# Sixteen more weight panels in block two by seven half-size products, weight sums made by adding transfers in DRAM

## The reference

```python
h = rms_norm_2(x, norm_g)
proj = h @ w_in                      # 1024 -> 4 branches and 4 x 1024 gates
y_a = chunked_spatial_gating(a_u, a_v, ...) * jax.nn.silu(a_z)
y_b = dsa_attention(b_q, b_c, b_qi, b_ki, b_wi, ...) * jax.nn.silu(b_z)
y_c = short_gated_conv(c_b, c_c, c_x, conv_w) * jax.nn.silu(c_z)
y_d = forgetting_attention(d_q, d_k, d_v, d_f, fox_b_f) * jax.nn.silu(d_z)
branch_d = jnp.einsum('nbsw,nwd->bsnd', jnp.stack([y_a, y_b, y_c, y_d]), w_branch)
g = jax.nn.sigmoid(gates.reshape(bsz, s, 4, d))
x + jnp.sum(g * branch_d, axis=2) @ w_out      # then a last rms norm
```

## Time and profile before

| | |
|---|---|
| median of 3 runs | 1111.67 us (1111.41 to 1111.82) |
| span of the profiled execution | 1109.4 us, 18066 instructions (its own time beyond the span is not on the page) |
| PE | 7344 matmuls, 1100.7 us busy |
| PEld | 931.1 us |
| DVE | 1195 instructions, 744.2 us busy |
| ACT | 851 instructions, 506.9 us busy |
| POOL | 40 instructions, 19.8 us busy |
| TensorE clock granted | 0.999 of full speed over the span |
| DMA | 121.09 MB, 109 GB/s as a mean |
| queue of SP (q1) | 109.88 MB, its packets took 29.7% of 16 engines' span |
| queue of POOL (q0) | 10.03 MB, 2.7% |

### The profile page before, as it was taken

The page is one execution under the profiler, slowest core; times in us unless marked ns, Lnnn a source line. Parts: engine busy times, 40 slices in busy tenths (PEclk is TensorE's granted clock), DMA queues, the critical chain, the costliest instruction groups (busy, mean ns, idle before and its releaser), DMA issues.

```text
span 1109.4 us, 18066 instructions
## 1 busy us (share of the span) xinstructions
PE 1100.7 (99%) x7344; PEld 931.1 (84%) x7344; DVE 744.2 (67%) x1195; ACT 506.9 (46%) x851; POOL 19.8 (2%) x40
## 2 busy tenths in 40 slices
PE   9999999999999999999999999999999999999997
PEld 8888888888888888878888887887789999999986
DVE  6875876864686247448789896447568677667853
ACT  7562354324675225533342434336544444444543
POOL 1000000000001001000000000000000000000000
PEclk9999999999999999999999999999999999999999
DMA  9543324432215433522223232231121322333241
GB/s 372 220 149 125 125 68 133 127 102 73 74 58 167 139 95 111 185 74 79 77 76 95 77 95 68 66 114 58 58 73 61 114 93 80 115 115 114 81 186 76
DMA packets 33618, 121.09 MB, mean 109 GB/s; under 512 B 3824, under 2 KB 3824, under 8 KB 33536
## 3 DMA queue, kind: packets, MB, share of 16 engines
q1 hardware_dynamic: 30672, 109.88, 29.7%
q0 software_dynamic: 2720, 10.03, 2.7%
q10 hardware_dynamic: 144, 0.03, 0.0%
HBM read 115.74 MB, written 4.19 MB: 108 GB/s over the span
## 4 chain that ended last, share of the span: by engine, by line
PE 98%; DMA 1%; DVE 1%; ACT 0%; SPq 0%; issue 0%; ACTq 0%
PE acc L1829 22%; PE acc L1831 21%; PE acc L1830 21%; PE acc L1841 2%; PE side L1841 2%; PE acc L1839 2%; PE side L1839 2%; PE acc L1837 2%; PE side L1837 2%; PE acc L2189 2%; PE side L1829 2%; PE side L1830 2%; PE side L1831 2%; PE side L2071 2%; PE side L1984 2%; PE side L2189 1%
## 5 line engine op out<-in xcount | busy, mean ns | idle before, releaser
L1160 DVE TENSOR_TENSOR w_lo<-raw,w_hi 128x1024 fp32r<-128x1024 f32 (+2 forms) x194 | 225.8, 1165 | 149.7 <-ACT w_hi L649 146.8
L1829 PE MATMUL acc<-hT_hi,w_hi 128*128 128x512 f32 x648 | 258.9, 400 | 0.0
L1831 PE MATMUL acc<-hT_hi,w_lo 128*128 128x512 f32 x648 | 252.8, 390 | 0.0
L1830 PE MATMUL acc<-hT_lo,w_hi 128*128 128x512 f32 x648 | 252.4, 390 | 0.0
L649 ACT ACTIVATE w_hi<-raw 128x1024 fp32r<-128x1024 f32 (+2 forms) x194 | 195.6, 1009 | 115.4 <-PE acc L1831 87.7
L1829 PEld LDWEIGHTS acc<-hT_hi,w_hi 128*128 128x128 f32 x648 | 121.9, 188 | 26.9 <-issue 2.9
L1831 PEld LDWEIGHTS acc<-hT_hi,w_lo 128*128 128x128 f32 x648 | 121.6, 188 | 26.1
L1830 PEld LDWEIGHTS acc<-hT_lo,w_hi 128*128 128x128 f32 x648 | 121.9, 188 | 23.6
L1829 PE MATMUL acc<-w_hi,hT_hi 128*128 128x512 f32 (+1 forms) x152 | 60.3, 396 | 0.0
L1831 PE MATMUL acc<-w_hi,hT_lo 128*128 128x512 f32 (+1 forms) x152 | 58.8, 387 | 0.0
L1830 PE MATMUL acc<-w_lo,hT_hi 128*128 128x512 f32 (+1 forms) x152 | 58.7, 386 | 0.0
(11 more groups left out here) (461 smaller groups left out, 2251.5 us busy)
## 6 DMA issues: line engine op xcount, KB each, us to landing
raw<-in_ga SPq DMA_DIRECT2D x32, 512.0 KB, 4.5
ada_raw<-in_ada SPq DMA_DIRECT2D x16, 512.0 KB, 11.5
raw<-in_wo SPq DMA_DIRECT2D x16, 512.0 KB, 3.5
raw<-in_br SPq DMA_DIRECT2D x16, 512.0 KB, 3.5
raw<-in_q SPq DMA_DIRECT2D x8, 512.0 KB, 3.5
raw<-in_u SPq DMA_DIRECT2D x8, 512.0 KB, 4.0
raw<-in_gp SPq DMA_DIRECT2D x8, 512.0 KB, 4.5
raw<-in_ada_w SPq DMA_DIRECT2D x8, 512.0 KB, 3.6
```

Of the source, the lines that this page charges most:

```text
L1160: nc.vector.tensor_tensor(out=lo[:, 0:width], in0=strip_of(k), in1=hi[:, 0:width].bitcast(f32), op=ALU.subtract).then_inc(lo_made, 1)
L1829: nc.tensor.matmul(ps, w[0], x[0], start=first, stop=False)
L1830: nc.tensor.matmul(ps, w[0], x[1], start=False, stop=False)
L1831: return nc.tensor.matmul(ps, w[1], x[0], start=False, stop=last)
```

## The change

- The 16 panels `dq`, `dk`, `bz`, `dz` become eight quads. Quad p has the steps `pa`, `pb`, `pd`, `pc` and seven products (84 matmuls of 256 columns): `pa` one or two of them, `pb` two, `pd` one, `pc` three, of which the middle one is the next quad's first. Quads 0 and 1 are q, 2 and 3 k, 4 to 7 z of branches b and d. ACT keeps four results of a quad, DVE adds four (`quad_add`). A quad carries two slots, `pb` slot 32 + 2p and `pc` slot 33 + 2p. `dv` moves ahead of the quads.
- All weight sums, of the 14 gate pairs and of the 8 quads, are made in DRAM by POOL's queue: `sum_weights`, eleven batches of two pairs. A batch is two copies from DRAM to DRAM, then four accumulating transfers in three waves with waits between. Batches 0 to 3 follow the clear of `u_pad`, 4 to 7 that of `attn[1]`, 8 to 10 the last cut of scores. SP loads the sums from `sums_kept` and the plain blocks from the input `st`. `combine` is gone.
- T1 and T2 are made at (`av`, 0) to (`au`, 2), and two new token sums T5, T6 at (`dv`, 0) to (`dv`, 2). T3 moves from (`ga`, 1) to (`ga`, 2). Some signs change.
- T5 and T6 take the room of y_a: after its last tile POOL writes `y_hi` and `y_lo` of branch a to `ya_kept` in DRAM (2 MB), and brings them back after the last `pc`; PE waits for that before the first `br` (`parked`).
- Branch d's scores start in slot 40, not 38, its last gates are applied at the first `br`. The z gates are spread over quads 5 to 7, `ga` 0 and `ga` 1 (`quad_exp`, `bound_gate`, `gate_sigmoid`, `quad_finish`).

The core of the diff:

```diff
-for kind in ("dq", "dk", "dv", "bz", "dz"):
-    ORDER += [(kind, j) for j in range(4)]
-for j in range(KT):
-    ORDER += [("ga", 4 * j), ("ga", 4 * j + 1), ("br", 2 * j), ("ga", 4 * j + 2), ("ga", 4 * j + 3), ("br", 2 * j + 1)]
+ORDER += [("dv", j) for j in range(4)]
+FIRST_PAIR, LAST_PAIR, QUADS = 2, 2 * KT - 1, 8
+for j in range(QUADS):
+    ORDER += [("pa", j), ("pb", j), ("pd", j), ("pc", j)]
+for j in range(2 * KT):
+    ORDER += [("ga", 2 * j), ("ga", 2 * j + 1), ("br", j)] if j < FIRST_PAIR else \
+        [("sa", j), ("sb", j), ("br", j), ("sc", j), ("sd", j)]
...
 def to_split(k):
+    if USED[k][0] in QUAD:
+        return {"pa": [k + 3, k + 4], "pc": [k + 2, k + 3]}.get(USED[k][0], [])
...
-    SCORES_AT[(1, 9, 19, 27)[_s // 4] + _s % 4 if _s < SPARSE else 38 + (_s - SPARSE) // 2].append(_s)
+    SCORES_AT[(1, 9, 19, 27)[_s // 4] + _s % 4 if _s < SPARSE else 40 + (_s - SPARSE) // 2].append(_s)
...
+            def sum_weights(batch):
+
+                st = dram["st"][SUM_BATCH * batch:SUM_BATCH * batch + SUM_BATCH]
+                kept = sums_kept[SUM_BATCH * batch:SUM_BATCH * batch + SUM_BATCH]
+                before = 96 * batch
+                if batch:
+                    pool.wait_ge(sums_made, before)
+                pool.dma_start(kept[:, :, 0:1536], st[:, :, 0:1536]).then_inc(sums_made, 16)
+                pool.dma_start(kept[:, :, 1536:2560], st[:, :, 1024:2048]).then_inc(sums_made, 16)
+                pool.wait_ge(sums_made, before + 32)
+                pool.dma_start(kept[:, :, 1024:1536], st[:, :, 1536:2048], accum_op=ALU.add).then_inc(sums_made, 16)
+                pool.dma_start(kept[:, :, 1536:2048], st[:, :, 0:512], accum_op=ALU.add).then_inc(sums_made, 16)
+                pool.wait_ge(sums_made, before + 64)
+                pool.dma_start(kept[:, :, 0:512], kept[:, :, 1024:1536], accum_op=ALU.add).then_inc(sums_made, 16)
+                pool.wait_ge(sums_made, before + 80)
+                pool.dma_start(kept[:, :, 512:1024], kept[:, :, 0:512], accum_op=ALU.add).then_inc(sums_made, 16)
+
+            for batch in range(4):
+                sum_weights(batch)
+
             pool.wait_ge(totals_made, 1)
             pool.wait_ge(level_x, 2)
             nc.gpsimd.memset(attn[1][:, :, :], 0.0).then_inc(attn_clear, 1)
+            for batch in range(4, 8):
+                sum_weights(batch)
...
+            for batch in range(8, NSUM // SUM_BATCH):
+                sum_weights(batch)
+            pool.wait_ge(y_made, 4)
+            ya = [t["a"][:, :, :].rearrange("p k s -> p (k s)").bitcast(f32) for t in (y_hi, y_lo)]
+            for n in range(2):
+                pool.dma_start(ya_kept[:, 2048 * n:2048 * n + 2048], ya[n]).then_inc(parked, 16)
+            pool.wait_ge(unit_used, STEP["pc", QUADS - 1] + 1)
+            pool.wait_ge(parked, 32)
+            for n in range(2):
+                pool.dma_start(ya[n], ya_kept[:, 2048 * n:2048 * n + 2048]).then_inc(parked, 16)
...
+            def quad_add(p, col, half, n):
+
+                dst = quad_place(p, col, half)
+                nc.vector.scalar_tensor_tensor(out=dst, in0=acc[quad_banks(p)[n]][:, 0:HALF], scalar=quad_scale(p, col), in1=dst,
+                                               op0=ALU.mult, op1=ALU.add).then_inc(part_added, 1)
...
+            def quad(k, kind, p):
+
+                w, ps = weights(k), acc[quad_banks(p)[0]]
+                if kind == "pa":
+                    if p == 0:
+                        quad_first(0)
+                    quarters(quad_bank(p, 1), w, 512, (quarter(hT_hi, 1, 0), quarter(hT_lo, 1, 0))).then_inc(unit_used, 1)
+                if kind == "pb":
+                    quarters(quad_bank(p, 2), w, 512, (t_hi[1], t_lo[1]))
+                    pe.wait_ge(part_kept, 4 * p + 1)
+                    quarters(ps, w, 0, (t_hi[2], t_lo[2]), first=False).then_inc(unit_used, 1)
+                    all_of_slot(SLOT_AT[k])
+                if kind == "pd":
+                    quarters(quad_bank(p, 3), w, 0, (quarter(hT_hi, 1, 1), quarter(hT_lo, 1, 1))).then_inc(unit_used, 1)
+                if kind == "pc":
+                    pe.wait_ge(part_kept, 4 * p + 2)
+                    if p == 0:
+                        pe.wait_ge(t_step, T_STEP[6, "lo"])
+                    quarters(ps, w, 0, (t_hi[6], t_lo[6]), first=False).then_inc(part_made, 1)
+                    if p + 1 < QUADS:
+                        quad_first(p + 1)
+                    all_of_slot(SLOT_AT[k])
+                    pe.wait_ge(part_kept, 4 * p + 3)
+                    quarters(ps, w, 512, (t_hi[5], t_lo[5]), first=False).then_inc(unit_used, 1)
```

More of the change, by code:

```diff
@@ L844, in copy_outer, with act_forget @@
                             side[use % 4][0:C, :].rearrange("p (n s) -> p n s", s=C), ACT.Copy).then_inc(outer_copied, 1)
+            def act_forget(slot):
+                if slot != FORGET_AT:
+                    return
+                act.wait_ge(fgt_abs, 1)
+                then(nc.scalar.activation(forget[:, 1, :], forget[:, 1, :], ACT.Exp, scale=-1.0))
+                nc.scalar.activation(forget[:, 1, :], forget[:, 1, :], ACT.Ln, bias=1.0).then_inc(fgt_ln, 1)
+                act.wait_ge(fgt_sum, 1)
+                nc.scalar.activation(forget_r[0:4, :], forget[:, 0, :], ACT.Copy, scale=-1.0).then_inc(fgt_hi, 1)
@@ new lines, in keep_first, with side_or_acc @@
+            def keep_first(p):
+                act.wait_ge(part_made, 2 * p + 1)
+                if p == QUADS // 2:
+                    act.wait_ge(cum_read, 1)
+                if p > 5:
+                    act.wait_ge(quad_gated, 2 * (p - 5))
+                nc.scalar.activation(quad_place(p, 0, 0), side_or_acc(p, 0), ACT.Copy, scale=quad_scale(p, 0))\
+                    .then_inc(part_kept, 1)
+            def side_or_acc(p, n):
+                return acc[quad_banks(p)[n]][:, 0:HALF]
@@ new lines, in quad_exp @@
+            def quad_exp(n):
+                p, col = QUADS // 2 + n // 2, n % 2
+                act.wait_ge(part_added, 4 * p + (4 if col else 3))
+                if col:
+                    act.wait_ge(part_kept, 4 * p + 4)
+                if n:
+                    act.wait_ge(quad_gated, n)
+                else:
+                    wait_freed(act, RESULT[GATE_ORDER[-1]])
+                nc.scalar.activation(silu_e2[:, :], z_d[:, n % 4, :], ACT.Exp, scale=-1.0).then_inc(silu_exp, 1)
@@ L846, in _, with quad_end @@
+            def quad_end(k, p):
+                if p + 1 < QUADS:
+                    keep_first(p + 1)
+                act.wait_ge(unit_used, k + 1)
+                nc.scalar.activation(quad_place(p, 1, 0), side_or_acc(p, 0), ACT.Copy, scale=quad_scale(p, 1))\
+                    .then_inc(part_kept, 1)
+                if p >= QUADS // 2:
+                    quad_exp(2 * (p - QUADS // 2))
             gates = 0
@@ L1199, in make_tokens @@
                     dve.wait_ge(t_step, T_STEP[1, "full"])
[L1200 to L1205 removed]
+                    then(nc.vector.scalar_tensor_tensor(out=full[2], in0=hi[1, 1], scalar=-1.0, in1=full[1],
+                                                        op0=ALU.mult, op1=ALU.subtract))
@@ L2136, in side_slot, with all_of_slot @@
                     ins.then_inc(mixed_made, 1)
+            def all_of_slot(slot):
+                side_slot(slot)
+                if slot == FORGET_AT:
+                    pe.wait_ge(exp_made, SPARSE)
+                    for t in range(TT):
+                        ins = nc.tensor.transpose(side[0][0:4, t * P:(t + 1) * P], forget_tok[:, 4 * t:4 * t + 4], ident[:, :])
+                    ins.then_inc(fgt_made, 1)
+                if slot == CUM_AT:
+                    pe.wait_ge(fgt_sum, 1)
+                    for t in range(TT):
+                        ins = nc.tensor.transpose(side[1][:, 4 * t:4 * t + 4], forget[:, 0, t * P:(t + 1) * P],
+                                                  ident[0:4, 0:4])
+                    ins.then_inc(cum_made, 1)
             pe.wait_ge(consts, 2)
@@ L2182, in _ @@
                 if (kind, j) in EARLIER:
+                    continue
+                if kind in QUAD:
+                    quad(k, kind, j)
                     continue
```

422 lines of the change are left out of this document (266 added, 156 removed).

## The result

The changed kernel takes 1130.92 us in the median of four runs (1129.65 to 1131.62), the kernel before 1111.7: 1.0171 times the time, 95% interval 1.0159 to 1.0183. It is 19 us slower. The forecast was slower, but by 7.3 us. The profiled execution has a span of 1129.1 us, 19.7 above the one of before. One fact belongs ahead of all comparisons: the changed kernel's time is not steady. Measured again on another chip it had a median of 1128.37 (1127.74 to 1131.53), while the kernel before stayed within 0.4 us.

What follows compares the result with a forecast made beforehand. PE, busy 99% of the span, was taken to bound the kernel. Its list's -6.8 plus waits of 2.0, 4.1 and 8 gave +7.3, 1119.0 us; own range 1114 to 1126, whole range 1106.5 to 1131.

Steps and rivals of the forecast that it cites:

- The waits that it named: PE's waits at the early token sums, the forget chain and branch d's slots: 2.0, 4.1 and 8 us, 14.1 together.
- rival (d): The forecast, with the head of the gate stage late too, or landings beyond 12.6 us: 1124 to 1131 us; chance 0.07.
- (a): Side work's slack covers the quads; slots cost about nothing, early and forget waits 2 us together: 1107 us; chance 0.20.
- (b): Branch d's slots free, but the early and forget waits in full, 6.1 us: 1111 us; chance 0.15.
- (c): POOL's queue late, above 42.6 us per batch of sums: 1146 us at the high end; chance 0.08.
- The list, -6.8: On PE, 672 matmuls of 256 columns replace 384 of 512: 80.6 us for 87.4, a gain of 6.8 us.
- T1 and T2, 2.0: Token sums made beside the top-k delay the third score's probabilities; PE waits 2.0 us, range 0 to 3.
- The forget chain, 4.1: At quad 1's last product PE waits for bank pa, emptied after ACT's chain: 4.1 us, range 2 to 5.
- The slots of branch d, 8: Forgetting attention in quads 5 to 7 and ga 0: about 2 us each, 8 us; range 3 to 13.
- The sums on POOL's queue, 0: Batches of DRAM sums take 28 us each, so later POOL work is in time: 0; high end 27 us.
- a landing doubles at worst: A load's landing beside a DRAM sum doubles at worst, to 9 us, inside 12.6, so no wait: 0.
- The later T3 and T4: In ga 2 they lengthen DVE's list by 0 to 3 us; nothing of PE's waits before the first br: 0.

Runs made afterwards that it cites:

- Run 5: Changed kernel with T1 and T2 made earlier, in bq 2 and 3, their low parts at av 0 and 1: 1126.96 us.
- run 13: Changed kernel with forget chain cut, T3 from DRAM, T1/T2 and attn[1] clear earlier; ACT's logarithm and exponential of b and d gates over 8 columns: 1111.7 us.
- run 10: Kernel before, with the eleven batches of adding transfers run on POOL's queue and their result unused: 1112.56 us.
- run 3: Changed kernel with T3 not made again but brought from DRAM, as the equal T6 written there earlier: 1125.4 us.
- Run 12: Changed kernel with four quads, forget chain cut, T3 from DRAM, T1/T2 and attn[1] clear earlier, and combine back on DVE for gate pairs: 1112.36 us.
- runs 2, 4 and 6: Changed kernel, respectively: without adding transfers, 1128.28 us; with the quads' same splits in another order, 1139.24 us; with four quads for eight, 1122.3 us.
- run 14: Changed kernel with forget chain cut, T3 from DRAM, T1/T2 and attn[1] clear earlier; gate work behind the slots in quads 5 to 7: 1117.93 us.

## Why the forecast was wrong

Its direction was right, its size was not: +7.3 forecast, +19 measured. The waits that it named came out nearly as priced, 14.2 us for 14.1. What failed is what the sum left out: above all the slow clock behind the waits, 6.2 us, and then the head of the gate stage, 3.0 us, which it put at nothing.

1130.9 lies just inside the whole range, at the end of rival (d), which had 0.07. That is mostly luck: of (d)'s two reasons the late head of the gate stage was there, but no landing was too late, and the larger part of the distance, the clock, is in no rival. (a) and (b) had the slots free and fell with the 8.2 us at the turns; (c) wanted batches over 42.6 us, and they took 39. Step by step:

- The list, -6.8: borne out. 672 matmuls were added and 384 went, the new ones 0.12 us apart where the clock is full.
- T1 and T2, 2.0: 1.85 waited, 2.1 lost, as priced. Run 5 takes it away.
- The forget chain, 4.1: 3.93 waited, at the place named, ACT's `part_kept` of `pc`.
- The slots of branch d, 8: 8.2. Right in sum, and partly by luck: I had about 2 us in each of quads 5 to 7 and in `ga` 0, and there were 0.3, 4.0, 2.0 and 1.9 in quads 4 to 7 and none in `ga` 0. The engine was only half right. I had DVE longer than PE and ACT with room; every one of these waits ends with ACT's copy, and run 13 shows that ACT's logarithm and exponential stand on the way to it. ACT did have room as a mean: it was busy for 12.2 us of the 17.9 from the second turn of slot 41 to that of slot 43. That did not help, since each of its steps waits for another engine.
- The sums on POOL's queue, 0: right, but nearer the edge than I took it, 39 us for 28. The traffic itself costs about 1 us (run 10), where I had 0; in the profiled run the early loss was 1.6. From the Trainium skill (DMA: Bandwidth & Descriptors, Queues, rings and completion order), where an engine goes round its queues packet by packet, I had worked out, as an estimate, that a landing doubles at worst. The trace does not bear this out: the median landing of the units of `i` went from 3.5 to 8.5 us, 2.4 times, and PE still waited for none.
- The later T3 and T4, "nothing of PE's waits": this step failed too. I looked at who needs T3 and T4, not at the `w_lo` queued behind them on DVE. 3.0 us, and clock behind it (run 3).
- The first tile of `dv` after `cz`, not looked at: 0.8. PE waited until DVE had read the last result of `cz` (L1469, 670.26 to 670.95 us). In the kernel before a panel of `dq` came next, and PE was in it already while DVE read (666.29 to 666.98). That `dv` lacks a free bank there was read from the code and not tried.
- The sum held waits only. This is the step that failed most: PE in the kernel before was always busy and ran at full clock; in the changed kernel three waits, of 3.9, 2.3 and 2.4 us, were each followed by 3.4 to 6.8 us at half of it. That is 6.2 us in the profiled run, none of it in any term. It also makes part of the spread, since the same wait has a fall behind it in one execution and none in another. No stretch of work at the lower level exists in the trace of before, so the price could only have been bounded; it was not even named.

With the clock, the head of the stage, the first tile of `dv` and the early loss the same ledger gives 7.3 + 6.2 + 3.0 + 0.8 + 1.6 = 18.9 of the 19.7.

## What to carry to other kernels

In a kernel that is bound by PE, a shorter list with more hand-overs is worth only what its waits leave: here 0.85 us for a pair of panels, against waits of 0.3 to 4 us each. Run 12, the best of the kernels here that compute the whole result, was no faster than the kernel before (1112.36 against 1111.54). Price a wait on a PE that was never idle with the slow stretch behind it, and look for what is queued behind a moved step on its engine, not only for who reads its result. Where an engine takes part in a chain with two others, its busy share does not tell whether it has room: ACT was busy for 12.2 us of 17.9 in the stretch with the longest waits, and every one of them ended with its copy:

```profile
758.30:776.20 17.90, 13.94 (x112) 13.23 (x112) 13.89 (x37) 12.21 (x28) 0.00 (x0) 1.00 0.31 104
```

(length, busy PE, PEld, DVE, ACT, POOL; clock, DMA share, GB/s.)

## What the runs showed of the hardware that I had not expected

- The granted clock fell to 0.50 behind idle times of 2.3, 2.4 and 3.9 us on PE in the changed kernel. The length of the wait alone does not decide it. After 2.32 us it fell in one profile of that kernel and not in the other; after the 1.8 us at the third sparse score it fell in runs 2, 4 and 6 and not in five other profiles; after 1.91 us at the last turn it fell in run 14 only. After one and the same wait of 3.93 us it was low for 6.8 us in one execution and 3.4 in another.
- An adding batch in DRAM (2.62 MB copied, 2.10 MB added in three waves) took 39 us in the changed kernel; a wave of two adds of 0.5 MB each 11 to 14, one alone 5.6 to 9.
- With such transfers beside it, PE sometimes waits 0.4 to 1.5 us with nothing shown that it waits for (cause open), and the time of the kernel before spreads over 3 us where it spread over 0.4.
